# Stick-breaking attention summed by parts: one sigmoid, no join, value products written turned and taken head by head

## What is computed

```python
def _stick_breaking(q, k, v):
    ...
        mask = kpos[None, :] < qpos[:, None]
        z = jnp.einsum('bhqd,bshd->bhqs', qb, k).astype(jnp.float32) * scale
        log_beta = jax.nn.log_sigmoid(z)
        log_1mb = jnp.where(mask, jax.nn.log_sigmoid(-z), 0.0)
        suffix = lax.cumsum(log_1mb, axis=3, reverse=True) - log_1mb
        a = jnp.where(mask, jnp.exp(log_beta + suffix), 0.0)
        return jnp.einsum('bhqs,bshe->bhqe', a.astype(v.dtype), v)

def _sb_layer(x, k, v, norm_g, w_in, w_out):
    proj = _rms(x, norm_g) @ w_in
    q, g = jnp.split(proj, [SB_W], axis=-1)
    o = _stick_breaking(q.reshape(b, s, SB_HEADS, SB_HEAD_DIM), k, v)
    o = o.reshape(b, s, SB_W) * jax.nn.silu(g)
    return x + o @ w_out
```

## Time and profile before

| what | value |
| --- | --- |
| median of 3 runs | 2392.08 us (2384.33 to 2392.08) |
| the profiled execution | 2385.55 us, of it 2383.7 us span from the first to the last instruction |
| granted TensorE clock | 0.997 of full speed over the span |
| busy share of the span | TensorE matmul 97%, VectorE 67%, ScalarE 43%, GpSimd 9% |
| the attention part, first scores to last value product | 1976.93 to 2280.18 us of the span |
| the tail | 2280.18 to 2383.70 us |

### The profile page before, as it was taken

How to read it: one execution, slowest core, us unless ns; L and a number is a source line. 1 busy time by engine, 2 the same in 40 slices (tenths; PEclk the granted TensorE clock), 3 DMA queues, 4 the chain that set the end, 5 groups by cost and what they waited for, 6 DMA issues and landing times.

```text
span 2383.7 us, 30315 instructions
## 1 busy us (share of the span) xinstructions
PE 2301.2 (97%) x12762; PEld 1234.2 (52%) x12762; DVE 1592.2 (67%) x2053; ACT 1017.9 (43%) x1482; POOL 208.1 (9%) x254
## 2 busy tenths in 40 slices
PE   7999999999999999999999988999999999989999
PEld 5445444444444444445544456654444446777765
DVE  6888867866766666787632389965534406989961
ACT  6255334322323223433322587732313216888841
POOL 0001030000000001623301100022000000000000
PEclk9999999999999999999999999999999999999999
DMA  5111010111110212103111000111231200010021
GB/s 187 36 37 69 1 36 36 61 46 71 58 49 36 71 71 71 38 1 142 36 71 36 32 5 1 62 46 36 71 141 36 72 1 1 1 36 1 1 89 54
DMA packets 50488, 116.02 MB, mean 49 GB/s; under 512 B 2418, under 2 KB 8107, under 8 KB 49968
## 3 DMA queue, kind: packets, MB, share of 16 engines
q1 hardware_dynamic: 48616, 105.40, 12.4%
q10 hardware_dynamic: 1736, 8.68, 0.9%
HBM read 101.49 MB, written 12.58 MB: 48 GB/s over the span
## 4 chain that ended last, share of the span: by engine, by line
PE 80%; DVE 11%; ACT 6%; issue 1%; DMA 1%; SPq 0%; DVEq 0%; ACTq 0%
PE PS L72 76%; PE PS L75 4%; ACT RG L81 3%; DVE R L93 2%; DVE RG L107 2%; ACT OV L84 2%; DVE R L101 1%; DVE RG L104 1%; DVE RG L101 1%; DVE RG L93 1%; ACT R L81 1%; DMA RG<-in_a_w_in 1%; DVE oss L110 1%; DVE dg L104 1%; DVE scl L110 0%
## 5 line engine op out<-in xcount | busy, mean ns | idle before, releaser
L72 PE MATMUL PS<-R,RG 128*128 128x512 f16 (+1 forms) x5184 | 1104.2, 374 | 9.4 <-DVE R L101 4.2
L72 PEld LDWEIGHTS PS<-R,RG 128*128 128x128 f16 (+1 forms) x5184 | 514.0, 104 | 592.8 <-issue 10.9
L72 PE MATMUL PS<-RG,R 128*128 128x512 f16 (+1 forms) x2904 | 631.2, 377 | 2.0 <-DVE R L101 1.7
L72 PEld LDWEIGHTS PS<-RG,R 128*128 128x128 f16 x2904 | 283.7, 98 | 330.0 <-issue 2.9
L81 ACT ACTIVATE RG<-RG,scl 128x4096 f16<-128x4096 f32 (+2 forms) x70 | 177.9, 2557 | 199.5 <-DVE scl L113 199.5
L101 DVE SCALAR_TENSOR_TENSOR RG<-RG,scl 128x4096 f16<-128x4096 f32 (+2 forms) x70 | 213.1, 3051 | 71.5 <-ACT RG L81 71.5
L101 DVE SCALAR_TENSOR_TENSOR R<-PS,scl,R 128x512 f32<-128x512 f32 (+1 forms) x227 | 159.2, 742 | 121.2 <-PE PS L72 98.8
L81 ACT ACTIVATE R<-PS,scl 128x512 f32<-128x512 f32 (+1 forms) x128 | 83.5, 685 | 326.4 <-PE PS L72 287.0
L107 DVE TENSOR_TENSOR_SCAN RG<-RG 128x127 f32<-128x127 f32 (+7 forms) x128 | 168.4, 1343 | 76.3 <-ACT RG L81 76.1
L110 DVE TENSOR_REDUCE scl<-RG 128x1 f32<-128x4096 f32 (+1 forms) x35 | 150.3, 4293 | 98.9 <-DMA RG<-in_w_ff 41.1
L72 PE MATMUL PS<-R,OV 128*128 128x64 f32 (+2 forms) x1456 | 193.7, 274 | 5.7 <-DVE R L93 5.4
(11 more groups left out here) (137 smaller groups left out, 1667.2 us busy)
## 6 DMA issues: line engine op xcount, KB each, us to landing
RG<-in_w_ff SPq DMA_DIRECT2D x16, 2048.0 KB, 8.5
RG<-in_a_w_in SPq DMA_DIRECT2D x8, 2048.0 KB, 8.7
xspill<-R ACTq DMA_DIRECT2D x2, 4096.0 KB, 16.0
RG<-in_w_kv SPq DMA_DIRECT2D x4, 2048.0 KB, 8.2
RG<-in_b_w_in SPq DMA_DIRECT2D x4, 2048.0 KB, 8.1
RG<-in_w_in SPq DMA_DIRECT2D x3, 2048.0 KB, 8.2
R<-in_x SPq DMA_DIRECT2D x8, 512.0 KB, 8.0
RG<-in_w_out SPq DMA_DIRECT2D x2, 2048.0 KB, 7.8
```

The lines of the kernel that those rows point to most:

```text
L72: return self.engine.matmul(*a, **k) if self.engine else Nothing()
```

## The change

It rewrites the attention part by the second form of the sum, and what hangs on it:

- V2 is replaced by the differences v_j - v_(j-1): during the Q products ScalarE issues, for each of 8 token tiles, DMAs that shift V2 by one row into `V2_BEFORE` (2 buffers in OV), and VectorE subtracts (`v_steps`).
- One sigmoid (of -z) per group is left. The mask goes into the scan: its second operand `later` is 0 where a key counts and 1 where it doesn't, and the second operation is max. The mask matmuls and the joins are gone.
- ScalarE's copy of the turned block becomes an activation, 1 - x.
- Value products are the other way round: 64 columns of V2 are stationary, the turned 128x128 block moves, and the result has head columns on partitions: an even head on 0 to 63, an odd one on 64 to 127. `values` lists, for each pair of heads, all blocks j of the even head, then all of the odd one.
- Groups of one head go two by two in a step (`sb_steps`, 54 steps). Score banks alternate between two pairs (0 to 3), transposes between banks 4 and 5, and value products use 6 and 7. A step first makes the scores of a later step, then for each half of each of its groups the transposes and a share of the value products of the step before.
- The gate is made turned (`product_t`), as is the gated result, so `gate_turn` and its transposes go. The sums of magnitudes of tiles 0 to 6 go through one matmul (`gate_bound`) in the place of GpSimd, tile 7 through another. The conversion of weight tile 40 moves from groups 22 to 29 to steps 28 to 35.

```diff
+        sb_steps = [[u] for u, (i, _) in enumerate(sb_groups) if i < 4]
+        sb_steps += [[u, u + 1] for u in range(len(sb_steps), len(sb_groups), 2)]
...
-            z = PS[:, 1024 * (u % 3):1024 * (u % 3) + len(hs) * sb_pitch(i)]
+            z = PS[:, 1024 * (u % 2):1024 * (u % 2) + len(hs) * sb_pitch(i)]
...
-                    for u, i, h, z in pair:
-                        mm = e.matmul(z[:, w - 128:w], identb[:, :], maskb[:, :], start=False, stop=True,
-                                      skip_group_check=True)
...
+            def turn(u, s):
+
+                _, at, n = sb_halves(u)[s]
+                b = banks.take_at(("tb", u, s), 4 + sb_units.index((u, s)) % 2)
+                e.wait_ge(*sig("scanned").at(u))
...
+                pairs = list(zip(pairs[:len(pairs) // 2], pairs[len(pairs) // 2:]))
+                return [(u, i, x, h, j) for two in pairs for u, x, h in two for j in range(i + 1)]
...
+                    r, q = 64 * (h % 2), 128 * (h % 8 // 2)
+                    mm = e.matmul(banks.ap(("pvb", i, g))[r:r + 64, q:q + 128], V2[:, j, 64 * h:64 * h + 64],
+                                  turned_at(u)[:, at:at + 128], start=(j == 0), stop=(j == i))
...
+            for z, step in enumerate([*sb_steps, []]):
+                if step and (0 < z < 20 or z > 20) and ahead:
+                    scores(ahead.pop(0))
+                if step == sb_steps[-1]:
+                    gate_bound(0, 7, 0)
+                work = values(sb_steps[z - 1]) if z else []
+                units = [(u, s) for u in step for s in range(len(sb_halves(u)))] or [None]
+                for y, unit in enumerate(units):
+                    if unit:
+                        turn(*unit)
+                    multiply(work[len(work) * y // len(units):len(work) * (y + 1) // len(units)])
...
+                        e.tensor_tensor(V2[:, t, :], V2[:, t, :], V2_BEFORE[t % 2], ALU.subtract).then_inc(
+                            *sig("v_steps").up(t))
...
+                for x in range(len(hs)):
+                    back = left(u)[:, w * x:w * x + w][:, ::-1]
+                    last = e.tensor_tensor_scan(back, back, later[:, 1024 - w:1024][:, ::-1], 1.0, ALU.mult, ALU.max)
...
+            gated(sb_steps[-3])
+            gated(sb_steps[-2])
+            gate_factors(0, 7)
+            gate_low(0)
+            gate_low(1)
+            gated(sb_steps[-1])
...
+                e.activation(turned_at(u)[:, at:at + n], banks.ap(("tb", u, s))[:, 0:n], ACT.Copy, bias=1.0,
+                             scale=-1.0).then_inc(*banks.empty([("tb", u, s)], sig("turned_b"), u, s))
```

More of the change, by code:

```diff
@@ L1014, in tensor, with gate_bound @@
                     product_t(36 + c, mi, n, h_rhs, ("q2", c, mi, n), ready=h_ready("b_norm_2", n))
[L1015 to L1030, removed]
+            for z, key in enumerate(G2[:14]):
+                _, c, mi, n = key
+                product_t(38 + c, mi, n, h_rhs, key, bank=z - 6 if z >= 12 else None)
+            def gate_bound(first, last, bank):
+                key = ("gate_bound", first)
+                b = banks.take_at(key, bank)
+                e.wait_ge(*sig("g_peak").at(last - 1))
+                e.wait_ge(*banks.free(key))
+                e.matmul(b[:, first:last], ones[:, :], col(24 + first, last - first), start=True,
+                         stop=True).then_inc(*full.up(*key))
             e.wait_ge(*sig("bank_dve").at("q2", 1, 3, 1))
@@ L1060, in scores @@
[L1060 to L1065, removed]
+                                mm = e.matmul(z[:, q:q + n], Q2[pr, a, h // 2, 128 * i:128 * i + 128],
+                                              K2[pr, b, h // 2, q:q + n], start=(a + b == 0), stop=(a == 1))
+                                if (a, q + n, two + 2) == (1, w, len(items)) and (len(groups) == 2 or h % 2):
+                                    mm.then_inc(*full.up("zb", u))
@@ new lines, in turn, with values @@
+            def turn(u, s):
+                _, at, n = sb_halves(u)[s]
+                b = banks.take_at(("tb", u, s), 4 + sb_units.index((u, s)) % 2)
+                e.wait_ge(*sig("scanned").at(u))
+                e.wait_ge(*banks.free(("tb", u, s)))
+                for x in range(0, n, 128):
+                    mm = e.transpose(b[:, x:x + 128], left(u)[:, at + x:at + x + 128], ident[:, :])
+                mm.then_inc(*full.up("tb", u, s))
+            def values(step):
+                pairs = []
+                for u in step:
+                    i, hs = sb_groups[u]
+                    pairs += [(u, x, h) for x, h in enumerate(hs)]
+                pairs = list(zip(pairs[:len(pairs) // 2], pairs[len(pairs) // 2:]))
+                return [(u, i, x, h, j) for two in pairs for u, x, h in two for j in range(i + 1)]
@@ L1066, in tensor @@
             scores([0])
             scores([1])
-            product_n(38, NT - 1, ("g2", NT - 1, 0), bank=6)
+            product_t(39, 2, 1, h_rhs, G2[14], bank=6)
             scores([2])
[L1070 to L1106, removed]
@@ new lines, in tensor @@
+            product_t(39, 3, 1, h_rhs, G2[15], bank=7)
+            ahead = [[u] for u in range(3, 22)] + sb_steps[22:]
+            for z, step in enumerate([*sb_steps, []]):
[9 more added lines that the diff above has]
+                    multiply(work[len(work) * y // len(units):len(work) * (y + 1) // len(units)])
@@ L2743, in scalar, with gate @@
-            for t in range(NT - 1):
-                gate_silu(t)
+            def gate(key, function):
+                _, c, mi, n = key
+                e.wait_ge(*full.at(*key))
+                e.wait_ge(*sig("w_scale").at(38 + c, 0))
+                return e.activation(GT[n][:, 512 * (4 * c + mi):512 * (4 * c + mi) + 512], banks.ap(key), function,
+                                    scale=w_scale(38 + c))
+            for key in G2[:14]:
+                gate(key, ACT.Silu).then_inc(*banks.empty([key], sig("bank_act"), *key))
@@ new lines, in one_minus @@
+            def one_minus(u):
+                i, hs = sb_groups[u]
+                g, held = hs[0] // 8, [("zb", u, q) for q in range(0, len(hs) * sb_pitch(i), 512)]
+                e.wait_ge(*full.at("zb", u))
+                e.wait_ge(*sig("zsc").at(1))
+                if u >= 5:
+                    e.wait_ge(*full.at("tb", u - 5, len(sb_halves(u - 5)) - 1))
+                e.activation(by_head(left(u), u), sb_scores(u), ACT.Sigmoid, scale=nsc[:, g:g + 1]).then_inc(
+                    *banks.empty(held, sig("one_minus"), u))
```

287 lines of the change are left out of this document (142 added, 145 removed).

## The result

The changed kernel takes 2497.6 us (median of 4 runs, 2494.76 to 2500.03) against 2390.69 for the kernel before (4 runs): ratio 1.0452, 95% interval 1.043 to 1.0475, **4.5% slower**. The forecast was 2378 us, its range ended at 2408. The profiled execution has a span of 2498.2 us, 114.5 more than before, and a mean granted clock of 0.977.

What follows compares the result with a forecast made beforehand. TensorE was taken as the largest load, with VectorE and ScalarE making it stumble. Attention +2.3 us and tail -10.0 gave -7.7 against the profiled 2385.55: 2378 us, range 2334 to 2408, the forecast's own 2366 to 2391.

Steps and rivals of the forecast that it cites:

- Differences of V2: During the Q products: 8 subtractions and 15 DMAs cost nothing; eight PSUM banks would cover 40 us of late landings.
- the case of no change: Whole kernel: a time within about 0.5% (12 us) of the kernel before, chance 0.38.
- Changes of the array's shape: Attention: runs of transposes 0.16 us each, values 0.15, scores 0.10, stops and first weight loads together adding 58.2 us.
- Rival 1: Attention: using half the columns costs no stop; attention 260.9 us, whole kernel 2333 us; chance 0.22.
- Value products at 0.11: Attention: turned value products stay at 0.11 us each, 126.7 us for 1152, no gain.
- Rival 2: Value products: weights aren't loaded behind a matmul of the same half, 0.055 us more per record; 2441 us, chance 0.10.
- Attention, 305.5 us: Attention after the change: 247.5 of work + 58.2 - 2.2 + 2.0 of waits, +2.3 us against 303.25.
- 2.0 us of waits: Attention: of TensorE's 35.2 us of waits before, 2 us are left with the second transpose bank.
- Rival 3: Attention: half of the 35.2 us of waits remain, with fewer score banks, +15.6 us; 2394 us, chance 0.13.
- Tail: After the attention: earlier first product, no gate transposes, no late step; -10.0 us from 103.52.
- (b): Tail: 48 gate transposes between output products go, saving 5.2 us.
- (c): Tail: one late step of 3.13 us, where others last 1.31, goes, saving 1.8 us.

Runs made afterwards that it cites:

- experiment 2: The changed kernel with each 127-row V2 shift cut into two DMAs of 122 + 5 rows: 2414.82 us.
- Kernel 4: kernel 1 with VectorE making the low half of each piece of weight tile 40 one step later: 2367.62 us, ratio 0.9921 to the kernel before.
- experiment 6: Kernel 4, head by head, with the transposes of two half tiles together, then their share of value products: 2333.67 us, ratio 0.9768 to the kernel before.
- kernel 1: The changed kernel with each 127-row V2 shift cut into two DMAs of 112 + 15 rows: 2382.61 us, ratio 0.9985 to the kernel before.

## Why the prediction was wrong, point by point

**The step that failed is "Differences of V2".** It counted 8 subtractions and 15 DMAs, found that their place had room, and set them at nothing. A landing of over 10 us was thought of, but two things were wrong. The landing was left open at "over 10 us" and the shape of the transfer not looked at, though the shape sets it: 127 rows of 4 KB, all on one engine, 0.157 us each. And the cover was read as if it were renewed: "eight PSUM banks would cover 40 us". The banks cover a delay once: TensorE waited 3.63 us in the first round and 11.7 to 17.8 in each of the seven others. Eight landings in a row of 19.93 us, each tied to a product of 5.2 us, cost by estimate 8 x 14.7 = 118 us less what is covered once; measured, the part ahead of the attention lost 114.2 us where the sum had nothing. The Trainium skill's rule on the number of engines (experiment 2) would have given the one engine beforehand.

With that fault alone mended, the kernel takes 2382.6 us: 4.6 above the forecast, and 0.15% below the kernel before, the case of no change that held 0.38. That it comes so near is in part luck: the attention was 5.4 us longer than the sum has it, because two errors of opposite sign partly cancel, as shown below.

**Changes of the array's shape** (+58.2 us) were nearly right. The rows had shown 0.10 for half the rows only; for half the columns the price is of the same kind, 0.295 for a pair of changes with its weight loads against 0.31, so some 55 us in all; it is this that eats most of what joins, mask and second sigmoid give back. The rule of the Trainium skill, TensorEngine Tiling, section Key Properties, that a change of the tiling mode drains TensorE, agrees with this: half the columns are charged too, 0.295 us a pair. **Rival 1** (no stop) falls.

**Value products at 0.11** were right for the order given, and so was the reason that no more could be had: neighbours want the same half. **Rival 2** falls: 8 records and a change hold 1.02 us, not 1.4. With it falls, for this case, the rule of the Trainium skill, TensorE: Matmul & The Clock Gate, section The mechanism, that weights load ahead only where the row group differs: all rows are in use here, and the records are 0.109 us apart.

**Attention, 305.5 us.** The changed kernel took 315.2, of which 4.2 are clock lost in tile 5, so 310.9 at full clock. Of those, 14.4 go with the waits in tile 5, against "2.0 us of waits" in the sum. This is the term that was mis-sized: I freed VectorE of 88 us of joins and did not look at the order of its queue, where one instruction that waits for ScalarE's last work of a step holds up the scans of the next. Without them it is 296.5, so the rest of the sum was 9 us too high. Kernel 4's timeline, added up from start to start, says where: waits are 0.4 us in place of 2.0; transposes with their changes 88.3 in place of 90.8; value products with theirs 144.7 in place of 150.0, mostly because runs in which the halves meet save by estimate 5.9 us (12 runs x 0.43, and 0.8 in the last run) and not 20 x 0.11 = 2.2; scores 52.4, forecast 52.3. Two heads of tile 7 take 7.82 us (1.40 of scores, 2244.12 to 2245.52, and 6.42 of the rest, both in experiment 6), forecast 7.9; two of tile 4 take 5.37 (2089.57 to 2094.94 in kernel 4), forecast 5.4.

**Rival 3** (waits stay, 2394 us) was right in its sign for the attention, and nearly in size (+15.6 against 13.8 + what hangs on them), but not by what it named: not fewer score banks, but VectorE's queue.

**Tail**, -10.0 us: measured -9.2. Its first product of 24 starts 1.7 us after the last values (2403.92 to 2405.61, 1 forecast, 4.15 before), so 2.5 are saved and not 3. The late step of the earlier trace rows is gone; at the same place, the seventh product, the transposes now hold 0.44:

```profile
2401.04 2.95 PE L72 MATMUL PS<-OV,R 128*64 128x128 f32 x29
...
2403.92 0.66 PE L75 MATMUL PS<-ident,R 128*128 128x128 f32 x4
...
2405.61 5.34 PE L72 MATMUL PS<-RG,R 128*128 128x512 f16 x24 [1.04 <-DVE R L93]
...
2439.05 0.60 PE L75 MATMUL PS<-ident,R 128*128 128x128 f32 x4
2439.49 5.34 PE L72 MATMUL PS<-RG,R 128*128 128x512 f16 x24
```

From the start of the first to the start of the last output product it is 84.4 us (to 2490.03) against 91.3 before (2284.33 to 2375.65): 6.9 less, where terms (b) and (c) together forecast 7.0. No experiment took these two apart.

## What to carry to other kernels

Price every DMA that a change adds by its shape before calling it hidden: how many rows, over how many engines, how long a row; 127 rows on one engine took a round of 19.93 us, 112 + 15 rows landed in under 4. A buffer of banks hides one delay, not a delay that comes with every step; compare the added wait with the step's length, and if it is longer, the step's length is what changes. And where products use only half of the array, the order decides: the same instructions head by head or in turn differed by 47 us, and fewer, longer runs between changes of shape by 34.

## What was not expected of the hardware

- A DMA of 127 rows of 4 KB within SBUF took a round of 19.93 us, 122 + 5 rows 9.75 us, 112 + 15 rows landed in 3.6 and 3.9 us.
- A small DMA behind such a one pays for it: 64 KB landed in 18.3 us instead of 1.9, and the four loads of `in_b_w_in` on the other queue took 10.3 us in the median, 8.4 in kernel 1 (what delayed them was not taken apart).
- With TensorE idle 12 of every 20 us the granted clock was 0.67 over 100 us, but it was back at 1.00 for the attention's first 110 us. The same waits of tile 5 passed at 1.00 in one execution and cost 4.2 us of clock in another.
- Two float32 matmuls on different halves of the columns, with different stationary values and into the same bank, run side by side: 0.055 us a record against 0.109. Even in head-by-head order, records overlap where the two halves meet inside a run: 0.38 us at each such place in tiles 2 and 3 of kernel 6.
